# A two-model kernel on one core: the second model's 16 meta tokens as one 48-column stationary operand, and one vector instruction per attention map

## The reference, cut to what matters

```
hn = rmsnorm(h, gain[l])
dq, dk, dv, dg, fq, fk, fv, ff, fg = split(hn @ w_in[l])      # columns: 8 blocks of 512, and 8
# four "diff" heads: two maps each, block-wise visible, a = softmax(s0) - lam * softmax(s1), a @ dv
s = (q @ k.T) * 0.125;  s = where(visible, s, -inf);  p = softmax(s)
# eight "forgetting" heads: causal, s += c[q] - c[k], c = cumsum(log_sigmoid(ff + bias)), p @ fv
h = h + concat(do * silu(dg), fo * silu(fg)) @ w_out[l]
```

## Time and profile before

| | |
|---|---|
| median of 3 runs (lowest, highest) | 1720.77 us (1715.64, 1721.52) |
| the profiled execution: its own time, its span | 1720.16 us, 1718.4 us |
| second model's two layers, in the span | from about 1292 us to the end |
| TensorE busy, over the span | 1615.2 us (94%) |
| DVE, ACT busy | 1221.8 us (71%), 1035.8 us (60%) |

### The profile page before, as it was taken

The page is one execution under the profiler, slowest core; times in us unless marked ns, Lnnn a source line. Parts: engine busy times, 40 slices in busy tenths (PEclk is TensorE's granted clock), DMA queues, the critical chain, the costliest instruction groups (busy, mean ns, idle before and its releaser), DMA issues.

```text
span 1718.4 us, 21553 instructions
## 1 busy us (share of the span) xinstructions
PE 1615.2 (94%) x8649; PEld 1356.6 (79%) x8649; DVE 1221.8 (71%) x1299; ACT 1035.8 (60%) x1236; POOL 61.6 (4%) x71
## 2 busy tenths in 40 slices
PE   5999999988889999999999999999989998899987
PEld 5877788888778888888888878888868886788866
DVE  3655555468568888888888888888885576555665
ACT  4644544356567776776767767677775446454463
POOL 0000000014000000000000000000000200003000
PEclk9999999999989999999999999999998999899999
DMA  7422555552359999899999999999996532346410
GB/s 251 147 99 92 187 186 174 193 192 94 105 188 334 384 320 353 315 385 359 342 331 307 409 317 356 338 333 380 324 310 182 106 114 74 60 88 134 123 40 38
DMA packets 133080, 389.31 MB, mean 227 GB/s; under 512 B 8694, under 2 KB 14266, under 8 KB 132844
## 3 DMA queue, kind: packets, MB, share of 16 engines
q1 hardware_dynamic: 132692, 387.15, 66.1%
q10 hardware_dynamic: 280, 0.70, 0.1%
HBM read 386.78 MB, written 1.05 MB: 226 GB/s over the span
## 4 chain that ended last, share of the span: by engine, by line
PE 82%; DVE 7%; ACT 7%; issue 3%; DMA 0%; ACTq 0%; POOL 0%; DVEq 0%
PE psum L359 26%; PE psum L361 24%; PE psum L360 24%; DVE wlo L192 3%; ACT whi L182 3%; PE psum L1541 1%; PE psum L1593 1%; PE psum L2260 1%; PE psum L1135 0%; ACT hh L1653 0%; PE psum L2105 0%; PE psum L418 0%; PE psum L2246 0%; PE psum L2151 0%; PE psum L1622 0%
## 5 line engine op out<-in xcount | busy, mean ns | idle before, releaser
L192 DVE TENSOR_TENSOR wlo<-raw,whi 128x2048 fp32r<-128x2048 f32 (+1 forms) x286 | 629.5, 2213 | 217.6 <-ACT whi L182 216.8
L182 ACT ACTIVATE whi<-raw 128x2048 fp32r<-128x2048 f32 (+1 forms) x286 | 525.9, 1847 | 235.3 <-PE psum L361 235.3
L359 PE MATMUL psum<-whi,xh 128*128 128x512 f32 (+1 forms) x1280 | 497.9, 389 | 18.6 <-DVE xl L2606 9.9
L361 PE MATMUL psum<-whi,xl 128*128 128x512 f32 (+1 forms) x1280 | 486.4, 380 | 0.0
L360 PE MATMUL psum<-wlo,xh 128*128 128x512 f32 (+1 forms) x1280 | 484.9, 379 | 0.0
L359 PEld LDWEIGHTS psum<-whi,xh 128*128 128x128 f32 x1280 | 242.4, 189 | 75.3 <-issue 13.3
L361 PEld LDWEIGHTS psum<-whi,xl 128*128 128x128 f32 x1280 | 242.0, 189 | 49.3
L360 PEld LDWEIGHTS psum<-wlo,xh 128*128 128x128 f32 x1280 | 242.8, 190 | 45.6 <-issue 0.2
L192 DVE TENSOR_TENSOR wlo<-raw_more,whi 128x2048 fp32r<-128x2048 f32 (+1 forms) x94 | 204.0, 2177 | 38.9 <-ACT whi L182 38.2
L182 ACT ACTIVATE whi<-raw_more 128x2048 fp32r<-128x2048 f32 (+1 forms) x94 | 171.4, 1827 | 53.4 <-PE psum L361 53.4
L359 PE MATMUL psum<-xh,whi 128*128 128x256 f32 (+2 forms) x552 | 165.8, 300 | 16.8 <-DVE wlo L192 15.3
(11 more groups left out here) (362 smaller groups left out, 1503.9 us busy)
## 6 DMA issues: line engine op xcount, KB each, us to landing
raw<-in_moe_w_down_dram SPq DMA_DIRECT2D x58, 1024.0 KB, 7.7
raw<-in_moe_w_gate_dram SPq DMA_DIRECT2D x43, 1024.0 KB, 6.3
raw<-in_moe_w_up_dram SPq DMA_DIRECT2D x41, 1024.0 KB, 5.6
raw_more<-in_moe_w_down_dram SPq DMA_DIRECT2D x30, 1024.0 KB, 7.4
raw<-in_w_in_dram SPq DMA_DIRECT2D x28, 1024.0 KB, 8.0
raw_more<-in_moe_w_up_dram SPq DMA_DIRECT2D x23, 1024.0 KB, 5.6
raw_more<-in_moe_w_gate_dram SPq DMA_DIRECT2D x21, 1024.0 KB, 6.5
raw<-in_moe_w_up_dram SPq DMA_DIRECT2D x23, 768.0 KB, 4.8
```

The source lines that it names most:

```text
L182: act.e.activation(self.whi[:, i % self.ns, 0:kt * n], self.place[self.slots[i]][:, 0:kt * n], ACT.Copy, scale=1.0).then_inc(self.s_hi)
L192: dve.e.tensor_tensor(self.wlo[:, i % self.ns, 0:kt * n], self.place[self.slots[i]][:, 0:kt * n], self.whi[:, i % self.ns, 0:kt * n].bitca ...
L359: pe.e.matmul(o, lh, rh, start=start, stop=False)
L361: return pe.e.matmul(o, ll, rh, start=False, stop=stop)
```

## The change

1. **Meta tile.** A new tile `xm` (128 x 8 x 48) holds the meta tokens' high halves in columns 0 to 15, zeros in 16 to 31 and the low halves in 32 to 47. `mm2` multiplies it by the high and by the low part of the weights, so two matmuls with 48 stationary columns do what three did; rows 0 to 15 and 32 to 47 of the result are added afterwards by a DVE instruction of 16 x 512. It is used for tile 0 of dv and fv in both layers and of the output projection in layer 0. POOL copies the halves into `xm`; the forgetting heads write theirs directly.
2. **Order.** In layer 0 the output projection takes its tiles as 1, 2, 0 in the first part (`TILES`), before it was 0, 1, 2.
3. **Scores.** Mask, scale and running maximum (a minimum, signs turned) come from one `tensor_tensor_reduce` for each of the two maps, with a mark for each; the exponential takes scale -1. TensorE's next scores wait for the second map's mark.
4. **fv, tile 0.** Before: ACT evicts, rounding and masking, and DVE subtracts. Now: ACT evicts to `fv0`, DVE adds the low rows, ACT rounds into `fvh`, DVE subtracts.

```diff
+TILES = ((1, 2, 0), (0, 1))
...
+    def mm2(pe, o, lhl, rh, rl, start, stop):
+
+        pe.e.matmul(o, lhl, rh, start=start, stop=False)
+        return pe.e.matmul(o, lhl, rl, start=False, stop=stop)
...
+                    if meta is not None and t == 0:
+                        pe.wait_ge(meta[1])
+                        ins = mm2(pe, psum[0:48, banks[t], 0:n], meta[0][:, k0 + k, :], wh[:, k, :], wl[:, k, :],
+                                  p == 0 and k == 0, last)
+                        continue
...
+        TS = TILES[l]
+        OUT = [(0, t, h) for h in range(2) for t in TS] + [(1, t, h) for t in range(lt, -1, -1) for h in range(2)]
...
+                        if t == 0:
+                            ins = mm2(pe, psum[0:48, banks[t], :], xm[:, kk, :], wh[:, k, :], wl[:, k, :], kk == 0, kk == 7)
+                            continue
...
+                    if rows[t][1] == NM:
+                        pe.wait_ge(m_copied.at(l, "d"))
+                        ins = mm2(pe, psum[0:48, bk, :], xm[:, kk, :], wh[:, k, :], wl[:, k, :], k == 0, k == 3)
+                        continue
...
-                pe.wait_ge(top2.at(l, u - 1, "s") if u else r_sin.at(l, 7))
+                pe.wait_ge(top2.at(l, u - 1, 1) if u else r_sin.at(l, 7))
...
-                act.e.activation(fvh[:, j, :], psum[:, 7 - j % 2, :], ACT.Identity, bias=0.0,
-                                 scale=1.0 if j else k2("meta")).then_inc(fv_out.end(l, j))
+                if j:
+                    act.e.activation(fvh[:, j, :], psum[:, 7 - j % 2, :], ACT.Copy, scale=1.0).then_inc(fv_out.end(l, j))
+                    return
+                act.e.activation(fv0, psum[:, 7, :], ACT.Identity, bias=0.0,
+                                 scale=k2("meta")).then_inc(fv_high.end(l))
+                act.wait_ge(fv_both.at(l))
+                act.e.activation(fvh[:, 0, :], fv0, ACT.Copy, scale=1.0).then_inc(fv_out.end(l, 0))
...
-                act.wait_ge(top2.at(l, u, "max"))
                 for a in range(2):
+                    act.wait_ge(top2.at(l, u, a))
                     ins = act.e.activation(sv[:, a, :], sv[:, a, :], ACT.Exp, bias=s2[0:m, u, a:a + 1],
-                                           scale=1.0, accum_out=s2[0:m, u, 2 + a:3 + a])
+                                           scale=-1.0, accum_out=s2[0:m, u, 2 + a:3 + a])
...
+                o = vvd[0:NM, 0, :]
+                dve.wait_ge(dv_out.at(l, 0))
+                dve.e.tensor_tensor(o, psum[32:32 + NM, 3, :], o, ALU.add).then_inc(dv_both.end(l))
...
+                if j == 0:
+                    src, o = fv0, fv0[0:NM, :]
+                    dve.wait_ge(fv_high.at(l))
+                    dve.e.tensor_tensor(o, psum[32:32 + NM, 7, :], o, ALU.add).then_inc(fv_both.end(l))
                 dve.wait_ge(fv_out.at(l, j))
...
+                if m == NM:
+                    dve.e.tensor_tensor(o, psum[32:32 + m, 6 + n % 2, :], o, ALU.add).then_inc(meta_low.end(part, h))
+                    dve.wait_ge(meta_low.at(part, h))
                 dve.e.tensor_tensor(o, psum[0:m, 6 + n % 2, :], o, ALU.add).then_inc(o_add.end(l, part, t, h))
...
+                mk, c = (k2("dmask", m), max(qi - 1, 0) * NT) if kind == "d" else (k2("fmask", m), qi * NT)
+                for a in range(2):
+                    dve.e.tensor_tensor_reduce(sv[:, a, :], psum[0:m, a, 0:nk], mk[:, c:c + nk], -0.125 if kind == "d" else -1.0,
+                                               BIG, ALU.add, ALU.min, s2[0:m, u, a:a + 1]).then_inc(top2.end(l, u, a))
...
+            def meta_pair(x_or_d, *marks):
+                n = 8 if x_or_d == "x" else 4
+                pool.wait_ge(m_copied.at(0, "zeroed"), *marks)
+                pool.e.tensor_copy(xm[:, 0:n, 0:NM], xh[:, 0:n, 0:NM].bitcast(F32)).then_inc(m_copied.end(l, x_or_d + "_high"))
+                pool.e.tensor_copy(xm[:, 0:n, 32:48], xl[:, 0:n, 0:NM].bitcast(F32)).then_inc(m_copied.end(l, x_or_d))
```

More of the change, by code:

```diff
@@ L77, in constants @@
     fm = np.where(pos[None, :] <= pos[:, None], 0.0, -BIG).astype(np.float32)
+    assert not dm[16, 0:NM].any()
     put(b, C2, "dmask", np.concatenate([dm[16:144], dm[144:272]], 1))
@@ L349, in body @@
                                                   ("fv", 2)) for j in range(n)]
-                  + [("out", l, 0, h, t) for h in range(2) for t in range(2 - l)]
+                  + [("out", l, 0, h, t) for h in range(2) for t in TILES[l][:-1]]
                   + [("out", l, 1, h, t) for t in range(2 - l, 0, -1) for h in range(2)]])
@@ L1835, in body @@
     s_sc, s_exp2 = steps("att_scores", *LU), steps("att_exps", *LU)
-    top2 = steps("att_top", *[(*lu, x) for lu in LU for x in ("s", "max")])
+    top2 = steps("att_top", *[(*lu, a) for lu in LU for a in range(2)])
     wts = steps("att_weights", *[(*lu, x) for lu in LU for x in (("inv", "lam", "p0", "a") if kind_of[lu] == "d" else ("inv",))])
@@ L1851, in body @@
     LT = [(l, t) for l in range(2) for t in range(2 - l, -1, -1)]
-    o_add = steps("out_added", *[x for l in range(2) for x in [(l, 0, t, h) for h in range(2) for t in range(3 - l)]
+    o_add = steps("out_added", *[x for l in range(2) for x in [(l, 0, t, h) for h in range(2) for t in TILES[l]]
                                  + [(l, 1, t, h) for t in range(2 - l, -1, -1) for h in range(2)]])
+    m_copied = count_on(ended_dense[0], [(0, "zeroed"), (0, "x_high"), (0, "x"), (0, "d_high"), (0, "d"), (1, "x_high"), (1, "x")])
+    dv_both, fv_high, fv_both = (count_on(old, [(0,), (1,)]) for old in ended_dense[1:4])
+    meta_low = count_on(ended_dense[4], [(part, h) for part in range(2) for h in range(2)])
     o_sqH = steps("out_squared", *[(*lt, h) for lt in LT for h in range(2)])
@@ L2013, in turned_in, with f_pair @@
             return 4 + k % 4, k // 4 * T if l else 0
+        def f_pair(u):
+            (qi, qo, m, nk), kind, i = units[u]
+            if qi == 0:
+                return xm[:, 4 + i, 0:NM], xm[:, 4 + i, 32:48]
+            return [t[:, 4 + i, qo - x0:qo - x0 + m] for t in (xh, xl)]
         def unit_f(t, i):
@@ L2153, in rope @@
                     yield
-            beside_dv(moving_steps(pe, ("dv", l), m3, [3, 4, 5], x, [[b_out.at(l, j)] for j in (3, 4, 5)]), rope())
+            beside_dv(moving_steps(pe, ("dv", l), m3, [3, 4, 5], x, [[b_out.at(l, j)] for j in (3, 4, 5)],
+                                   meta=(xm, m_copied.at(l, "x"))), rope())
             def beside_d():
@@ L2439, in finish @@
                     act.wait_ge(f_w.at(l, u))
-                    act.e.activation(xh[:, 4 + i, qo - x0:qo - x0 + m], fw[:, u % 2, 0:m], ACT.Copy,
-                                     scale=1.0).then_inc(f_xh.end(l, u))
+                    act.e.activation(f_pair(u)[0], fw[:, u % 2, 0:m], ACT.Copy, scale=1.0).then_inc(f_xh.end(l, u))
                     return
@@ L2723, in pool @@
                 pool.wait_ge(*layers[0].ends)
+            def meta_pair(x_or_d, *marks):
[3 more added lines that the diff above has]
+                pool.e.tensor_copy(xm[:, 0:n, 32:48], xl[:, 0:n, 0:NM].bitcast(F32)).then_inc(m_copied.end(l, x_or_d))
+            if l == 0:
+                pool.wait_ge(x(7))
+                pool.e.memset(xm[:, :, :].bitcast(F32), 0.0).then_inc(m_copied.end(0, "zeroed"))
+            meta_pair("x", m_x.at("low") if l else x(7))
             for r in range(9):
```

47 lines of the change are left out of this document (16 added, 31 removed).

## The result

The changed kernel takes **1710.64 us** (median of 4 runs, 1709.22 to 1711.99) against 1720.67 us for the kernel before beside it (4 runs, 1715.64 to 1721.52): ratio 0.9943, 95% interval 0.9929 to 0.9956. That is 10.0 us, where 7.5 were forecast (1713.0, range 1707.5 to 1718). The profiled execution has a span of 1710.2 us.

A forecast was written before the change was run, and what follows sets the result against it. TensorE, busy 94% of the span, was taken as the bound, except where it waits for ACT and DVE chains. dv -3.5, fv -0.6, scores -2.2, output projection -1.4 and POOL +0.2 gave -7.5 us: 1713.0 us, range 1707.5 to 1718.

The forecast's parts named there:

- dv, -3.5: dv, both layers: eight matmuls saved a layer arrive almost fully because TensorE is busy without a break; -3.5 us.
- fv, -0.6: fv, both layers: a longer wait and a later ACT/DVE chain leave 0.2 to 0.3 us a layer; -0.6 us taken.
- TensorE needs it for the values it began at 1434.21: fv: values wait for the late copy `aT`, beginning about 1434.0 instead of 1433.3.
- bound of -1.9: fv: the favourable end, 0.93 us arriving in both layers if the SBUF copy costs next to nothing.
- Scores, -2.2: Forgetting units' scores on DVE: fused instructions shorten the chains to two stalls, -1.1 us a layer, -2.2 in both.
- Output projection, -1.4: Layer 0's output projection, four meta tiles of four saved matmuls: -1.4 us, between -3.8 and -0.4.
- The third tile: Layer 0's output projection, first meta tile: TensorE shortened by 0.93 us, about 0.56 us arriving at the next wait.
- the end of the layer: Layer 0's last two output tiles: 1.86 us saved buy nothing; four additions in a row start layer 1 0.5 us later.
- the sixth tile: Layer 0's output projection: runs mostly at the lower clock, 0.427 us a matmul, so the saving is -1.3 us.
- POOL, +0.2: POOL's zeroing and copies: the two of layer 1 beside a conversion TensorE waits on cost 0.2 us, bounds 0 and 1.
- The clock: Rival, chance 0.20: new TensorE idle time brings two or three lower-clock stretches, +4.5 us, 1717.5.
- All matmuls in full: Rival, chance 0.17: all saved matmuls arrive, 11.1 us, with 2.2 and 0.7 more making 14 us; 1706.5.

The follow-up runs named there:

- run 5: The changed kernel with dv's first tile by three matmuls a step and without the add behind it: 1712.91 us, ratio 0.9961.
- run 3: The changed kernel with fv's first tile by three matmuls a step and its evictions as before: 1711.35 us, ratio 0.9944.
- run 4: The changed kernel with fv's first tile by three matmuls a step, the longer chain (eviction, add, second copy) kept: 1709.61 us, ratio 0.9937.
- run 2: The changed kernel with the old scores instructions, the saved matmuls kept: 1713.73 us, ratio 0.9956.
- run 1: The kernel before with the fused scores alone, all its matmuls as they were: 1716.45 us, ratio 0.9974.
- run 6: The changed kernel with the last two output tiles of each layer by three matmuls a step and one addition each: 1708.52 us, ratio 0.9931.
- run 7: The changed kernel with the last-but-one tile's two additions ahead of the norm chain in layer 0: 1708.91 us, ratio 0.9926.
- run 8: The changed kernel with the meta tile first again in layer 0's output projection, first part: 1713.45 us, ratio 0.9951.
- run 12: run 11 plus sixteen matmuls of 512 columns in the wait ahead of layer 0's first transposes: 1705.77 us, ratio 0.9916.
- run 10: The kernel before with twelve filling matmuls ahead of each layer's first output tile: 1712.55 us, ratio 0.9956.
- run 11: The changed kernel with twelve filling matmuls, layer 0's early additions, and each layer's last tile by three matmuls into 16 rows with one addition: 1705.51 us, ratio 0.9917.
- run 9: The changed kernel with twelve filling matmuls into the free bank ahead of each layer's first output tile: 1707.47 us, ratio 0.9933.

## Why the forecast was right, and where not

The time and the direction were right, and the mechanisms of three terms held. That the sum came as near as it did (7.5 for 10.0) is in part luck: two errors, 1.3 us too little for fv and 0.8 too much for the output projection, partly cancelled, and the clock, which the sum left out, has a share in the 10.0.

- **dv, -3.5:** right in size and place: 3.7 in the ledger, and 3.7 by the positions of run 5.
- **fv, -0.6: the step that failed.** "TensorE needs it for the values it began at 1434.21" is wrong. The copy `aT` made at 1432.02 serves the unit after; the values run a unit behind it. So nothing waited for the late chain, and the second half arrived whole, 1.9 us in both layers. Runs 3 and 4 show it: the chain alone costs 0 to 0.3 us, the matmuls 1.0 a layer. The forecast's own bound of -1.9 was the truth. I had taken two things that stand 2 us apart in time for a chain, and not looked up the copy's buffer number or the unit that each belongs to.
- **Scores, -2.2:** right. 2.4 measured, 1.2 a layer by run 2, 2.3 by run 1. The price of an instruction was 0.05 us too high. In the chain the unit with 272 keys counts 0.4 us and the two with 144 keys 0.4 each, where I had 0.55, 0.28 and 0.28. So the size came out right by luck, too: by the cheaper instructions the unit with 272 keys should have given 0.66, and the forecast did not see that `oxd` behind them would wait for POOL.
- **Output projection, -1.4:** -0.6 without the clock. The third tile gave 0.43 for 0.56, the end of the layer cost 0.76 for 0.5, and the sixth tile gave 0.93 because it ran at the full rate; the other 1.6 us of its shift are the clock's. Runs 6 and 7 show the additions as the cause at the end of the layer.
- **POOL, +0.2:** the copies cost nothing, in any trace with the order (1, 2, 0). Run 8 shows it as a cost of 0.5 us where its cover is gone.
- **The clock.** As a rival it was to take 4.5 us back. Its price was too low: twelve matmuls at 0.427 instead of 0.232 us make 2.3 us, not 1.6 to 2, and with it two or three stretches 4.7 to 7. In fact the clock took 2.2 us back in layer 1 and gave 3.0 in layer 0. Which stretches fall in one execution isn't settled by the program: the same instructions behind 1385 took 3.0 us more in the traces of runs 4, 7, 8 and 12 than in those of the changed kernel and of run 3, and up to there runs 4, 7 and 8 issue in this model what the changed kernel issues. The net of -0.8 us in one pair of profiles is thus not shown to be a property of the change. Two kinds of stretches do keep to the program. That of the sixth tile stands in the traces of the kernel before and of run 1, and in none of the eight kernels with the saved matmuls and no filling. Those behind the two stalls of 5 us stood in every trace without the filling, and went with it (in layer 1 of runs 10 to 12 they moved into the filling).
- **All matmuls in full** (1706.5) was wrong for the reason given: fv's first halves and the last two tiles, 3.7 us together, went into waits.

What stays open: why the slow stretches 27 and 41 us after the filled stall went too in run 10 and not in run 9, and how much of the change's 10 us is its effect on the clock. Without stretches in the ledger it is 9.2 us, between both filled kernels 5.1, and one profile each doesn't reconcile them. The mean granted clock over each run is on record as well, and bears on this. Of the 36 runs of the kernel before, 26 stand at 0.971 to 0.975 and take 1720.6 to 1724.0 us, ten at 0.977 to 0.979 and take 1715.5 to 1720.3; the changed kernel's four stand at 0.975 to 0.979. Runs at 0.979 differ by 6.3 us (1716.1 and 1709.8, two each), those at 0.977 by 7.6 (1719.6, four, and 1712.0, one). So some 2 to 4 of the 10 us go with the clock; whether the change brings the higher clock about isn't shown.

## What to carry to other kernels

Before a late copy or conversion is put on the path, find its reader by unit and buffer, for in a software pipeline the instruction that starts next often reads what was made a stage ago. A merged result that takes two additions saves on TensorE and costs on DVE and on its bank: it pays inside a busy stretch and loses at a stage's end. Where TensorE idles for some 5 us ahead of full tiles, fill that with matmuls into a free bank before judging edits that save single ones: by the positions it gave 3.6 us in the changed kernel and 7.6 in the one before. And where an instruction gets shorter, see what else the next one waits for: of 0.66 us saved on DVE ahead of `oxd`, 0.28 did not arrive, since `oxd` then waited for POOL.

## What the runs showed of the hardware that was not expected

- A matmul with 48 stationary columns follows at 0.23 us, like one with 128; with 16 rows as the output it was no faster (run 11).
- The fused instruction over 272 PSUM elements follows at 0.37 us and over 144 at 0.24: about 1.0 ns an element and 0.1 us beside.
- Twelve filling matmuls begun 1.4 us after the last work ran at the full rate in layer 0 of run 9 (3.01 us), and in its layer 1, 1.0 us after the last work (3.00 us). In layer 1 of runs 10, 11 and 12 they ran at the lower one (5.0, 5.5 and 5.5 us) and ended the stall themselves. The tile behind them was fast, but the layer then won only 0.2 to 0.4 us by it, against 2.5 in run 9.
